# Two up-projection pairs' products in another order, and mean squares summed and spread in other banks

## The reference, cut to what matters

```
x = x + einsum('bse,ed->bsd', y_mix, w_out[l])          # 1024 tokens, 1024 features
h = rms_norm(x, norm2_g[l])                              # x * rsqrt(mean(x*x, -1) + eps) * g
u = causal_dwconv(einsum('bsd,df->bsf', h, w_up[l]), ffn_conv_w[l])   # 6144 columns
gate, up = split(u, 2, axis=-1)
x = x + einsum('bsf,fd->bsd', gelu(gate) * up, w_down[l])
```

## Time and profile before

| | us |
|---|---|
| median of 3 runs | 1708.43 (1707.66 to 1709.9) |
| the profiled execution | 1707.96 |
| its span, first to last instruction | 1706.2 |
| TensorE busy in it | 1671.9 (98%) |
| VectorE busy | 1259.1 (74%) |
| ScalarE busy | 780.5 (46%) |
| GpSimd busy | 449.6 (26%) |

### The profile page before, as it was taken

The page is one execution under the profiler, slowest core; times in us unless marked ns, Lnnn a source line. Parts: engine busy times, 40 slices in busy tenths (PEclk is TensorE's granted clock), DMA queues, the critical chain, the costliest instruction groups (busy, mean ns, idle before and its releaser), DMA issues.

```text
span 1706.2 us, 20965 instructions
## 1 busy us (share of the span) xinstructions
PE 1671.9 (98%) x7556; PEld 1380.9 (81%) x7556; DVE 1259.1 (74%) x1490; ACT 780.5 (46%) x1047; POOL 449.6 (26%) x270
## 2 busy tenths in 40 slices
PE   7999999999999999999999999999999999999998
PEld 6888878888887888888888788887888887888786
DVE  6577772258999888888887789888828836777654
ACT  5566551235754434343434354454432327566531
POOL 4222222200005555455544000004523341300000
PEclk8999999999999999999999999999999999999999
DMA  7111112143423222222222884752322231020351
GB/s 262 50 37 49 37 50 71 41 174 104 143 75 99 74 86 91 81 74 86 85 88 75 286 306 140 255 191 69 105 87 61 68 105 31 6 81 26 111 218 72
DMA packets 161095, 176.96 MB, mean 104 GB/s; under 512 B 13566, under 2 KB 114692, under 8 KB 161028
## 3 DMA queue, kind: packets, MB, share of 16 engines
q1 hardware_dynamic: 158724, 167.67, 30.3%
q10 hardware_dynamic: 2304, 8.39, 1.3%
HBM read 140.38 MB, written 35.65 MB: 103 GB/s over the span
## 4 chain that ended last, share of the span: by engine, by line
PE 83%; DVE 10%; ACT 4%; issue 2%; DMA 1%; SPq 0%; POOL 0%; DVEq 0%; ACTq 0%
PE ps L941 29%; PE ps L2502 25%; PE ps L2456 16%; PE ps L2744 5%; PE ps L2729 3%; PE ps L2778 1%; PE ps L2701 1%; DVE pt_lo L2309 1%; DVE prob L2266 1%; PE ps L2580 1%; PE ps L2717 1%; ACT pt_hi L1592 1%; DVE square_dve L1693 1%; ACT scr L1540 0%; DVE xs L2084 0%
## 5 line engine op out<-in xcount | busy, mean ns | idle before, releaser
L965 POOL TENSOR_TENSOR w_lo<-w_raw,w_hi 128x1024 fp32r<-128x1024 f32 x52 | 134.6, 2590 | 629.8 <-ACT w_hi L1072 629.8
L2502 PE MATMUL ps<-hop_hi_P,wop_hi_P 128*128 128x512 f32 x672 | 262.5, 391 | 4.7 <-DVE u L1910 3.3
L2502 PE MATMUL ps<-hop_hi_P,wop_lo_P 128*128 128x512 f32 x672 | 261.5, 389 | 0.0
L2502 PE MATMUL ps<-hop_lo_P,wop_hi_P 128*128 128x512 f32 x672 | 261.5, 389 | 0.0
L971 POOL TENSOR_TENSOR wop_lo_P<-pair_sum,wop_hi_P 128x512 fp32r<-128x512 f32 x90 | 136.6, 1518 | 354.3 <-ACT wop_hi_P L1083 354.3
L941 PE MATMUL ps<-h_hi,w_hi 128*128 128x512 f32 x720 | 224.1, 392 | 5.5 <-DVE h_lo L1678 4.0
L941 PE MATMUL ps<-h_lo,w_hi 128*128 128x512 f32 x720 | 222.6, 391 | 0.0
L941 PE MATMUL ps<-h_hi,w_lo 128*128 128x512 f32 x720 | 222.4, 390 | 0.0
L941 PEld LDWEIGHTS ps<-h_hi,w_hi 128*128 128x128 f32 x720 | 135.2, 189 | 35.1 <-issue 7.5
L941 PEld LDWEIGHTS ps<-h_hi,w_lo 128*128 128x128 f32 x720 | 135.7, 189 | 28.4
L941 PEld LDWEIGHTS ps<-h_lo,w_hi 128*128 128x128 f32 x720 | 135.7, 189 | 28.4
(11 more groups left out here) (363 smaller groups left out, 3346.9 us busy)
## 6 DMA issues: line engine op xcount, KB each, us to landing
pair_raw<-in_w_up SPq DMA_DIRECT2D x48, 512.0 KB, 4.7
w_raw<-in_w_in SPq DMA_DIRECT2D x46, 512.0 KB, 3.9
dn_raw<-gu_park SPq DMA_DIRECT2D x84, 256.0 KB, 3.8
dn_raw<-in_w_down SPq DMA_DIRECT2D x60, 256.0 KB, 3.0
gu_park<-up_cv SPq DMA_DIRECT2D x24, 512.0 KB, 2.6
out_raw<-in_w_out SPq DMA_DIRECT2D x30, 256.0 KB, 3.0
x_tok<-in_x SPq DMA_DIRECT2D x4, 1024.0 KB, 8.1
x_park<-xs SPq DMA_DIRECT2D x1, 4096.0 KB, 14.3
```

What stands on the lines that cost most here:

```text
L965: nc.gpsimd.tensor_tensor(lo[:, :], raw[:, :], hi[:, :].bitcast(f32), ALU.subtract).then_inc(w_lo_done, 1)
L2502: mm = nc.tensor.matmul(dst, w[q][:, k, :], x[q][:, k, :], start=a, stop=b, skip_group_check=True)
```

## The change

**TensorE.** The order of the first products changes from P1/0, P2/0, P1/1, P5/0, P2/1, P6/0, P5/1, P7/0, P6/1, P4/0, P3/0, P7/1 to P1/0, P2/0, P1/1, P5/0, P2/1, P5/1, P6/0, P7/0, P6/1, P4/0, P7/1, P3/0. The first sum of squares is now two groups: 4 one-column products of the DVE total of squares 0 to 3 between P2/0 and P1/1, and 16 of squares 4 to 7 behind P1/1 (12 before, all behind P1/1). The second group of 16 moves from behind P2/1 to behind P6/1. The spread moves from behind P6/0 to behind P4/0, four products into the d bank of pair 0 and four into that of pair 1. The sums of squares go to `ps[3]` instead of `ps[2]`.

**DVE.** `half_squares(1)` is gone. The combination for P4 (`hop_add("P4")`) now waits for square number 15. C22/0 waits for the copy of the factor. Several low parts, U2/1, U3/0 and U2/2 are at other places; the low part of P7/1 comes from POOL to DVE, that of P3/0 goes to POOL.

**ACT.** The cast for P5/1 comes directly behind `first_sum` of pair 1, ahead of those for P6 and P7; squares 12 to 15 come behind these; the factor is copied in two instructions.

The core of the diff:

```diff
-        FIRST_TURNS = (("P1", 0), ("P2", 0), ("P1", 1), ("P5", 0), ("P2", 1), ("P6", 0), ("P5", 1), ("P7", 0), ("P6", 1),
-                       ("P4", 0), ("P3", 0), ("P7", 1), ("P4", 1), ("P3", 1), ("P1", 2))
-        BY_VECTOR = FIRST_TURNS.index(("P7", 1))
+        FIRST_TURNS = (("P1", 0), ("P2", 0), ("P1", 1), ("P5", 0), ("P2", 1), ("P5", 1), ("P6", 0), ("P7", 0), ("P6", 1),
+                       ("P4", 0), ("P7", 1), ("P3", 0), ("P4", 1), ("P3", 1), ("P1", 2))
+        BY_VECTOR = FIRST_TURNS.index(("P3", 0))
...
+                if the(k, 0):
+                    part_low("P3", k)
+                elif known(k, 1):
                     part_low("P7", k.plus(1))
...
+            first_sum(Pair(0, 1))
+            part_high("P5", Pair(0, 1))
+            part_high("P6", Pair(0, 0))
+            both_high("P6")
+            both_high("P7")
+            act.wait_ge(x1_parked[1], 16)
+            part_high("P7", Pair(0, 0))
             for j in range(12, 16):
                 square(OUT, j)
-            first_sum(Pair(0, 1))
-            both_high("P6")
-            part_high("P6", Pair(0, 0))
+            act.wait_ge(x1_parked[0], 64)
+            both_high("P4")
+            part_high("P6", Pair(0, 1))
+            part_high("P4", Pair(0, 0))
+            part_high("P7", Pair(0, 1))
+            part_high("P3", Pair(0, 0))
             norm_root(2)
-            both_high("P7")
-            part_high("P5", Pair(0, 1))
-            act.wait_ge(x1_parked[1], 16)
-            part_high("P7", Pair(0, 0))
             both_high("P3")
             act.wait_ge(rb_done, 2)
-            nc.scalar.copy(rstd_row, ps[3][:, :].rearrange("p (j t) -> p j t", j=2)).then_inc(rstd_spread, 1)
-            part_high("P6", Pair(0, 1))
-            act.wait_ge(x1_parked[0], 64)
-            both_high("P4")
-            for q in ("P4", "P3"):
-                part_high(q, Pair(0, 0))
+            for j in range(2):
+                nc.scalar.copy(rstd_row[:, j:j + 1, :], ps[1 + 2 * j][:, T2].unsqueeze(1)).then_inc(rstd_spread, 1)
...
-            half_squares(1)
             hop_low("P5", (1,))
             first_low("P5", 0)
+            first_low("P2", 1)
+            pair_sums(Pair(0, 1), (0,))
             hop_add(*t3)
             hop_add("P6", lambda h: part_of("B11", h), lambda h: hop_raw("P7", h), ALU.add)
-            half_squares(2)
-            first_low("P2", 1)
-            half_squares(3)
+            first_low("P5", 1)
             dve.wait_ge(x1_parked[0], 64)
+            dve.wait_ge(x1_square, OUT.square(16))
             hop_add("P4", lambda h: part_of("B21", h), lambda h: hop_raw("P6", h), ALU.subtract)
+            first_low("P6", 0)
             hop_low("P6")
-            first_low("P6", 0)
-            dve.wait_ge(root_done, 2)
-            V.reciprocal(rstd[:, :], small[:, 8:16]).then_inc(rstd_done, 1)
-            pair_sums(Pair(0, 1), (0,))
+            pair_sums(Pair(0, 1), (1,))
             hop_low("P7")
-            first_low("P5", 1)
             dve.wait_ge(x1_parked[1], 16)
             first_low("P7", 0)
             second_sum(Pair(0, 0))
-            pair_sums(Pair(0, 1), (1,))
-            hop_low("P3")
             first_low("P6", 1)
+            half_squares(2)
+            half_squares(3)
             hop_low("P4")
             first_low("P4", 0)
+            dve.wait_ge(product, nth("P7", Pair(0, 0)))
+            from_first(Pair(0, 0), u3)
+            pair_sums(Pair(0, 1), (2,))
+            dve.wait_ge(root_done, 2)
+            V.reciprocal(rstd[:, :], small[:, 8:16]).then_inc(rstd_done, 1)
+            second_sum(Pair(0, 1))
+            hop_low("P3")
+            first_low("P7", 1)
...
             def third_sums(k):
-                dve.wait_ge(product, nth("P7", k))
-                from_first(k, u3)
+                if the(k, 0):
+                    dve.wait_ge(rstd_spread, 2)
+                    dve.wait_ge(product, nth("P5", k))
+                else:
+                    dve.wait_ge(product, nth("P7", k))
+                    from_first(k, u3)
...
                 scale(k, "up")
+                if the(k, 1):
+                    second_sum(k.plus(1))
                 taps(k, 0)
                 if the(k, PAIRS - 1):
                     slice_low(DOWN, 4)
-                if known(k, 1):
+                if known(k, 1) and not the(k, 1):
...
+            pe.wait_ge(x1_squares, squared(OUT, 4))
+            total_squares(0, [square_at(OUT, 0)[2]], last=False)
             run("P1", two)
-            pe.wait_ge(x1_squares, squared(OUT, 5))
-            total_squares(0, [square_at(OUT, 0)[2]] + squares_of(1)).then_inc(ms_done, 1)
+            pe.wait_ge(x1_square, OUT.square(8))
+            total_squares(0, [square_at(OUT, j)[2] for j in range(4, 8)], first=False).then_inc(ms_done, 1)
             pe.wait_ge(product_added, OUT.added(14))
             run("P5", one, True)
             pe.wait_ge(s1c_done, 2)
             run("P2", two)
-            pe.wait_ge(x1_squares, squared(OUT, 7))
-            total_squares(4, squares_of(2) + squares_of(3)).then_inc(ms_done, 1)
+            run("P5", two)
             run("P6", one, True)
-            pe.wait_ge(rstd_done, 2)
-            spread(ps[3]).then_inc(rb_done, 1)
-            run("P5", two)
             pe.wait_ge(sums_done, sums("U2", one))
             run("P7", one, True)
-            pe.wait_ge(rstd_spread, 1)
             run("P6", two)
+            pe.wait_ge(x1_squares, squared(OUT, 6))
+            total_squares(4, squares_of(2) + squares_of(3)).then_inc(ms_done, 1)
+            pe.wait_ge(sums_done, sums("U3", one))
+            run("P4", one, True)
+            pe.wait_ge(rstd_done, 2)
+            spread(ps[1][:, T2], range(4))
+            spread(ps[3], range(4, NT)).then_inc(rb_done, 1)
+            pe.wait_ge(sums_done, sums("U2", two))
+            run("P7", two)
+            pe.wait_ge(sums_done, sums("C22", one))
+            run("P3", one, True)
```

45 lines of the change are left out of this document (21 added, 24 removed).

## The result

The changed kernel takes 1727.77 us (median of 4 executions, 1726.01 to 1729.58), the kernel before 1708.12 (1707.66 to 1709.9, 4 executions in the same call). The ratio is 1.011, with an interval of 1.0095 to 1.0125: slower, by 19.6 us where 11.8 were forecast. The time lies outside the forecast range of 1716 to 1723.5. The profiled execution of the changed kernel took 1726.01 us, 1724.2 of it the span.

The account below looks back on a forecast made before the run. TensorE was taken as the bound, with VectorE as full in this stretch. New stalls 14.2 us, less old 3.8, plus 1.7 for products and 0.1 for an interruption, gave 12.2; 11.9 taken, forecast 1720.2 us, range 1716 to 1723.5.

Parts of the forecast that it names:

- The hold of ScalarE: ScalarE's cast for P5/1 waits 5.7 us for product P5/0, delaying squares 12 to 15; P4's combination starts 7.75 us later.
- The longest new wait: TensorE stalls 6.5 us before P6/0, at about 500 us, until VectorE delivers a low part of the tokens.
- The wait for the root: VectorE runs out of work at 512.7 us and waits 2.7 us for the norm's root.
- The stall of 2.4 us before P7/0: TensorE, done with P6/0 at 503.4 us, waits 2.4 us before P7/0 for VectorE's work, done at 505.8.
- the stall before P4/1: The old kernel's 0.80 us wait of TensorE for U3/1, expected to go because P3/0 now stands ahead.
- the price list: Costs taken from the old trace: 2.72 us for each product on TensorE, 0.218 us for each one-column product.
- the forecast's stall before P1/3: TensorE waits 1.7 us before P1/3 for the taps of pair 1, which end at 549.3 us.
- GpSimd's part: VectorE instructions lengthened beside GpSimd's, carried over unchanged; bounds 2.2 us less or 2.2 us more.
- The stall of 3.6 us before P1/2: TensorE reaches P1/2 at 530.3 us and waits 3.6 us for the taps of pair 0.
- Eight one-column products: TensorE sums squares with 20 instead of 12 one-column products ahead of P5/0: 1.74 us more.
- the freed halving: The 1.14 us that VectorE saves without halving squares 4 to 7, counted as nothing because waits consume it.
- the rival in which the order works as it reads: Three old TensorE stalls go and the P5/1 cast holds nobody: 1706.4 us, not slower; chance 0.04.

Follow-up runs that it names:

- e3: Changed kernel with 27 unread matmuls of 512 columns added in TensorE's wait before P6/0: 1725.2 us, ratio 1.01.
- e2: Changed kernel with ScalarE's squares 12 to 15 and token casts ahead of the P5/1 cast again, VectorE's P5/1 low part behind P4's combination: 1719.22 us, ratio 1.0055.
- e10: Kernel of e1 with 12 of the 16 one-column products in each group replaced by 12 wide matmuls: 1708.71 us, ratio 0.9997.
- e8: Changed kernel with unread wide matmuls added: 8 within the two groups of 16, 27 before P6/0, 10 before P1/2: 1727.51 us, ratio 1.0108.
- e4: Changed kernel with VectorE's halving of squares 4 to 7 back, so 8 instead of 16 one-column products behind P1/1: 1724.2 us, ratio 1.0086.
- e11: The kernel before, unchanged, profiled a second time: 1710.08 us, span 1708.3.
- e9: Kernel of e5 with the norm at its old place and some VectorE and ScalarE instructions moved, the changed order of products kept: 1716.95 us, ratio 1.0045.
- e12: Kernel of e9 with ScalarE's casts and VectorE's sums reordered to suit the products, whose order stays: 1713.01 us, ratio 1.0018.
- e1: Kernel before with only squares 4 to 7 summed directly by TensorE and their halving on VectorE gone: 1714.84 us, ratio 1.003.
- e6: Kernel of e1 with four unread wide matmuls set between the one-column products of each group of 16: 1716.53 us, ratio 1.0046.
- e13: Kernel before with squares after the first four in rounded format, summed directly by two-column products, all three halvings gone: 1709.61 us, ratio 1.0005.
- e14: Kernel before with two-column products of rounded squares in place of one-column ones, all three halvings kept: 1707.76 us, ratio 0.9991.
- e5: Changed kernel with the edits of e2 and e4 together: 1718.6 us (three executions), ratio 1.0056.

## Why the prediction was right in direction and wrong in size

Against the rows of the changed kernel, counted from P1/0 (the forecast's own times less 472.17):

| | forecast | measured | difference so far |
|---|---|---|---|
| combination for P4 starts | 24.3 | 27.5 | +3.2 |
| P6/0 starts | 28.4 | 31.7 | +3.3 |
| P7/0 starts | 33.6 | 37.8 | +4.1 |
| C22/0 starts | 48.5 | 54.3 | +5.8 |
| taps of pair 0 end | 61.7 | 69.2 | +7.5 |
| P1/3 starts | 77.1 | 85.2 | +8.1 |

**What held.** The hold of ScalarE and its place: the cast for P5/1 is held by the product P5/0, ScalarE idle until 490.33, the squares behind it. The longest new wait: 6.45 us against 6.5, before P6/0, released by a token low part. The wait for the root: 2.78 against 2.7. The 16 matmul records more of the 8 one-column products (7572 on the page, 7556 in the earlier trace rows). That VectorE loses its lead and the rest of the span gives nothing back: TensorE is busy for 40.00 of 40.00 us from 560 on. The stall of 2.4 us before P7/0 is 0.85 in the changed kernel and 2.14 in e3, where P6/0 isn't slow. e2 shows the hold, with what it brings behind it, to be 10.0 us by the times and 7.6 by P1/3. Not held, at no cost to the time: the stall before P4/1 (0.80 before), which was to go, is 0.59.

**The step that failed** is the price list: "a product 2.72 us", used for every product, with one-column products at 0.218 us whatever their number. It is a price at full clock. The changed kernel pays 0.8 us more in the group of 16 that ends at 485.04 and 2.2 more for P5/0 (3.2 with what follows; the first two rows of the table), 0.85 at P6/0, 1.6 at P4/0, which takes 4.31 us and stands ahead of the spread, and about 0.5 at P1/2, whose slow 5.02 us hide the forecast's stall before P1/3. That is 6.2 of the 8.1 us. e10 shows the cause for the groups. For the wait it is e3 and e8, where it was filled and P6/0 ran at full clock, beside the changed kernel and e4, where it wasn't and P6/0 was slow. The rows from which the prices came carry a granted clock of 1.00 in each stretch, but I asked neither what would lower it, nor whether other executions had the same; the times of the kernel before run up to 1709.9 us, 2 us above the profiled one, and e11 shows one way in which they differ. A range with the 6.2 us in it and GpSimd's bound of 2.2 would have reached to about 1729 (1720.2 + 6.2 + 2.2).

**A term near its bound.** GpSimd's part was carried over unchanged, with 2.2 us more as its bound. It came to 1.8, the rest of the 8.1: VectorE's pair sums at 525.46 and 532.22 take 1.79 and 1.72 us, where one alone takes 0.69 and the one of 511.73 before took 0.78.

**A cause given too narrowly.** The stall of 3.6 us before P1/2 (measured 4.32) was put down to the late factor. In the changed kernel the factor is in the chain: just ahead of C22/0 VectorE waits 2.78 us for the root and 3.03 for the copy (1.5 in the forecast; the slow P4/0 ahead of the spread adds its 1.6). But with the factor back at 503 us (e9, e12) the stall is still 3.9 to 4.3, and other waits have taken the place of these two. The new order of products puts VectorE's work for pair 1 ahead of pair 0's C22/0, 5.7 us later than before in e12, and GpSimd adds to the stretch behind it. So an early factor alone would not have removed this stall; that the order of products makes it is the reading that is left, and no run changed that alone. That the forecast's stall was within 0.7 us of the measured one says little for its reason.

**The terms of the change.** Eight one-column products were charged with 1.74 us and the freed halving with nothing. Alone (e1) they cost 5.5 us by P1/3, of which 4.7 are the clock behind both groups of 16, and at full clock 0.8 (e10). And the rival in which the order works as it reads, 1706.4, asked for nothing but that the cast for P5/1 hold nobody. In e12 it holds nobody and P5/1 waits for nothing, and the time is 1713.0, in part by the clock (half from 494.5 to 498 and from 525 to 532), in part by the stall before P1/2: that rival was missing a condition.

What stays open: how many one-column products lower the clock. Behind groups of 16 unrounded ones it fell in 10 of 12 cases when they stood behind P2/1 or P6/1 and in all six when they stood ahead of P5/0 (e6 and e8, with wide matmuls between them, among both); behind 12 in one of two; behind 8 in none of four. Whether it falls differs between executions of one kernel (e11), so single profiles can't say more. Nor was it tried whether a cheaper sum of the squares repairs the changed kernel itself.

## What to carry to other kernels

Before a price is taken from a row, read the granted clock of its stretch, and ask what the change does to it: here a wait of several microseconds, or a run of matmuls with few columns, made the product behind it cost nearly twice, on top of the wait. In a stretch in which two engines are full, an order is judged by what each in-order stream has to wait for, instruction by instruction; here, moving work to the other engine moved the wait (e13, e14). And where a kernel's own executions differ by more than the effect that is to be explained, profile it twice before building on one of them. An experiment's gain, too, is to be looked up where the edit is: of e3's 2.5 us, 1.6 lay ahead of it.

## What the runs showed of the hardware

- At half clock (granted 0.5, 1.2 GHz) the matmuls of 512 columns follow each other by 0.43 us instead of 0.23, and a product of 12 takes 4.1 to 5.3 us where most or all of it lies in such a stretch. I had not expected this inside a kernel whose TensorE is busy for 97% of the span.
- One-column products keep TensorE busy by its busy share and still lower its clock: in e1 it was busy for 8.00 of the 8.00 us at 0.57. With twelve wide matmuls in place of twelve such products it stayed at 1.00 (e10), with four among sixteen it did not (e6). Two-column products in the rounded format did it too: behind 32 of them P6/0 took 5.01 us at a granted 0.53 (e13).
- A product with 128x128 weights and one or two columns takes 0.218 us unrounded (two matmul records) and 0.11 in the rounded format (one): 0.11 for each record, the same for one column as for two.
- A stretch at half clock also lay behind waits of only 1.80 (e8), 2.05 (e5) and 2.10 us (e14). Behind the stalls of 0.7 to 1.7 us of the kernel before none was seen in either of its profiles.
- VectorE's 128x512 sum of two SBUF inputs takes 0.69 us alone and up to 1.79 beside a GpSimd instruction (changed kernel at 525.46; 1.71 and 1.75 in e12).
